# Transformer block and mixer block on one core: the grid pooling of the D rows moves from GpSimd to VectorE, and two small steps of the A rows move to ScalarE

## The chip, the cores and the metric

The kernel runs on one core of one Trainium2 chip. The metric is the device time of one execution in microseconds (us), here the median of three runs. Engines are named as the profile names them: PE is TensorE, DVE is VectorE, ACT is ScalarE, POOL is GpSimd, SP is the engine that issues the DMAs.

## What is computed

Two blocks in a row on one sequence of 1024 tokens, width 1024, all in float32. The first block is a feed-forward layer, an attention and state-space mixer, a second feed-forward layer and an embedding gate; the change does not touch it. The second block is the mixer that the change is about:

```
proj = h @ w_in                       # 11 slots of 512: va za bb bc bv zb ca cg zc dv zd
ya   = rglru(va)                      # A rows: two 4-tap convolutions, gates, two scans
yb   = bb * conv3(bc * bv)            # B rows
yc   = silu(ln(conv31(ca * sigmoid(cg)))) @ c_pw + c_pw_b    # C rows
p    = pool_grid(dv)                  # D rows: box mean over a 16 x 64 grid, minus the token
yd   = (p @ d_w + d_b) * d_scale      # per group of 128 channels
out  = concat(ya*silu(za), yb*silu(zb), yc*silu(zc), yd*silu(zd)) @ w_out

# pool_grid: channel group ct = 0..3 has a window w = 2, 4, 8, 16 in both directions
total = sum of g[r0:r1, c0:c1],  r0, r1 = clip(r - w/2), clip(r + w/2), same for columns
mean  = total / ((r1 - r0) * (c1 - c0));   result = mean - u

# rglru, per direction: r, ig = sigmoid(xc @ w + b); a = exp(-8 r softplus(-lam))
# b = sqrt(1 - a^2) * ig * xc;   h = a * h + b, forward and backward over the tokens
```

## The kernel before

Channels lie on the 128 partitions and tokens along the free axis, so a slot of 512 channels is four rows of 128 x 1024, and the function `mixer` of each engine loops over these with `ct` = 0 to 3. There is no scheduler: each engine's program is written out by hand, in the order in which its instructions run, and `Signal` objects (`mm` for PE, `ac` for ACT, `ve` for DVE, `po` for POOL) give the semaphore values to wait for. An engine that waits holds back everything that stands behind it in its program.

**PE.** A product of a float32 weight block with the activations is done as three products of split values (high and low part), 24 matmuls of 128x512 for each half (512 tokens) of a row. `plane` issues the two halves of one or more rows. For one ct the order is va, dv, cg (three rows, all first halves and then all second halves), ca, the gate products of direction 0 (`gates(0, ct)`, on XC0), bc, bv, the gate products of direction 1 (on XC1), bb, zb, za, the product `dw` of the pooled D rows (on DV), zd; then the next ct. For ct = 0 the first five rows come half by half (`first_planes`). After ct = 3 come four rows zc, and then the output products.

**PSUM banks.** The ring `banks` has eight banks, taken in PE's order, so a product waits for the reader of the product eight takes before it. What matters here: bb waits for the ACT copy of bc, zb for DVE's multiplication `pb` with bv, and the first half of zd waits for DVE's multiplication `bb` with the first half of bb.

**Weights.** Each weight unit (128 x 1024) is loaded to one of three RAW slots by SP, then ACT writes the high half and DVE the low half of one of five WS slots (`halves`, called by `release`). The low half of a unit is made at that place of DVE's program where the unit five before it is released; it waits for ACT's high half, and that for PE to be done with the unit five before. At the start of a ct from 1 on, DVE's program makes three of them in a row, for the units that follow va, dv and cg in their slots, and the last cannot be made before PE has ended the second half of cg. So DVE's work on a ct is held until then.

**DVE, one ct.** (1) The two 4-tap convolutions XC0 and XC1 of the A rows: a TENSOR_SCALAR for the first tap and three SCALAR_TENSOR_TENSOR. (2) UU, the product of ca and the gate of cg. (3) `convolve(n)`: the next n of the 31 taps of the C rows' convolution, each a SCALAR_TENSOR_TENSOR on CV (128x1024); the taps are filler, spread over the ct, and the rest follows at its end. (4) `gates(0, ct)`: GG, then a wait for ACT's exponential and tanh, RG = (x+1)*RG (`gv1`), x = 1-RG (`gv2`), RG = (RG-2)*RG (`gv3`), a wait for ACT's square root, GG = GG*RG; then the scan YY (`y1`). (5) five taps, weights, `pb`, weights, `gates(1, ct)`, five taps, the scan `y2`, YY + RG, the 3-tap convolution of the B rows, four taps, `bb`. (6) weights, the gate rows zb and za, eight taps, the bias and scale of `dw`, the gate rows zd, the rest of the taps.

**ACT, one ct.** Copies VA, DV and the bc row out of PSUM, sigmoids, in `gates` the exponential, the tanh and the square root, and the Silu of the z rows.

**POOL.** Its only work of note is the pooling of the D rows (function `gpsimd`, lines 2950 to 2991), once per ct, after ACT's copy of dv into DV. It zeroes the column borders of D0, copies DV between them, adds along columns by doubling (ct + 1 adds), then adds 2 * 2^ct shifted rows one after the other into a zeroed tile, multiplies by the two reciprocal counts and subtracts DV in place:

```
            for o in range(-hw_, hw_):
                lo_, hi_ = max(0, -o), min(16, 16 - o)
                e.wait_ge(po("col", ct, o - 1))
                if hi_ > lo_:
                    tt(dst[:, lo_:hi_, :], dst[:, lo_:hi_, :], src[:, lo_ + o:hi_ + o, :], ALU.add).then_inc(*po.inc("col", ct, o))
```

In the rows of the profile DVE's and ACT's instructions carry the lines of small helpers: L1826 is `tt` of DVE (TENSOR_TENSOR), L1830 and L1831 `ts` (TENSOR_SCALAR), L1834 `stt` (SCALAR_TENSOR_TENSOR), L1837 `scan`, L1048 `act`, L360 a matmul of PE, L2954 `tt` of POOL.

Of the kernel before, what the change touches and what calls it, by code (L numbers as in the profile page):

```python
# [142 lines left out]
def build(nc, t, plan):  # L143
# [900 lines left out]
    def scalar(e):  # L1044
# [593 lines left out]
        def mixer():  # L1638
            for ct in range(4):
                us = [w.take() for _ in range(3 if ct else 5)]  # L1640

# [20 lines left out]
                if ct:  # L1662
                    for h in range(2):
                        va_copy(h)
                        if h:
# [13 lines left out]
                else:  # L1679
# [141 lines left out]
    def vector(e):  # L1821
# [1594 lines left out]
```

## Time and profile before

| | before |
|---|---|
| median of three runs | 3488.39 us (3485.23 to 3490.15) |
| the profiled execution's own time | 3490.11 us |
| its span | 3487.2 us |
| TensorE clock granted, mean | 0.977 |
| PE busy | 3303.1 us, 95% |
| DVE busy | 1923.3 us, 55% |
| ACT busy | 1063.6 us, 30% |
| POOL busy | 146.8 us, 4% |

The page's shares are means over the whole program. The mixer is the stretch from about 2670 to 3250 us of the span, and there the engines stand otherwise, so it is read by its own timeline. In a timeline row the first number is the start in us from the span's start, the second the length, and xN says that N like instructions were merged; instructions of one engine overlap a little, so intervals between starts are used for sums. In square brackets stands the idle time of the engine ahead of the row and what ended it. The ct before which a time lies can be told from POOL's rows: its adds of ct = 1, 2 and 3 begin at 2816, 2947 and 3086 us.

### The profile page before, as it was taken

What the parts mean: (1) busy time and instruction counts of PE and PEld (TensorE: products, weight loads), DVE (VectorE), ACT (ScalarE), POOL (GpSimd) and SP (SyncE); (2) the same over time, 40 slices, a digit from 0 to 9 for tenths busy, and PEclk for the clock granted to TensorE, in tenths of its full rate; (3) what the DMA queues carried; (4) which work ended last, traced back from release to release, by engine and by line L of the source; (5) the groups of instructions that cost most, each with busy time, mean ns of one, the idle gap of its engine ahead of it and who ended that gap; (6) DMA issues with size and microseconds to landing.
All of it is one profiled execution on the core that took longest, in us unless ns stands there. A gap on an engine that the chain in (4) does not pass through costs nothing.

```text
span 3487.2 us, 37191 instructions
## 1 busy us (share of the span) xinstructions
PE 3303.1 (95%) x15338; PEld 2669.8 (77%) x15338; DVE 1923.3 (55%) x3176; ACT 1063.6 (30%) x1547; POOL 146.8 (4%) x72
## 2 busy tenths in 40 slices
PE   8999999999999999989999999999999899898897
PEld 7888888877987877777778888888676677676686
DVE  4323322266768678786542222222767777878535
ACT  3121121224232566563231111111444322322412
POOL 0000000000000000000000000000001031251000
PEclk9999999999999999999999999999999999998998
DMA  4211211212433430014111111111112111112141
GB/s 146 74 61 61 73 61 49 73 57 101 129 102 120 151 110 13 13 43 161 45 37 49 49 49 49 49 43 49 49 55 84 67 48 69 37 52 97 61 151 49
DMA packets 86872, 246.95 MB, mean 71 GB/s; under 512 B 8368, under 2 KB 22064, under 8 KB 85168
## 3 DMA queue, kind: packets, MB, share of 16 engines
q1 hardware_dynamic: 86704, 244.58, 20.2%
q8 instruction: 121, 1.98, 0.2%
q14 instruction: 47, 0.39, 0.0%
HBM read 200.51 MB, written 44.04 MB: 70 GB/s over the span
## 4 chain that ended last, share of the span: by engine, by line
PE 77%; DVE 16%; ACT 5%; issue 2%; DMA 1%; DVEq 0%; SPq 0%; ACTq 0%
PE PS L360 75%; DVE CV L1834 2%; PE PS L365 2%; DVE XC L1834 1%; DVE X L1834 1%; DVE WS L1826 1%; DVE HELD L1869 1%; ACT WS L1048 1%; DVE RG L1834 1%; DVE XS L1834 1%; DVE GG L1826 1%; ACT PT L1048 1%; DMA RAW<-in_W 1%; DVE TMP L1834 1%; ACT RG L1048 1%
## 5 line engine op out<-in xcount | busy, mean ns | idle before, releaser
L360 PE MATMUL PS<-XS,WS 128*128 128x512 f32 x8352 | 1963.6, 396 | 76.1 <-DVE TMP L1826 24.3
L360 PEld LDWEIGHTS PS<-XS,WS 128*128 128x128 f32 x8352 | 1587.3, 191 | 437.9 <-issue 87.3
L360 PE MATMUL PS<-HS,WS 128*128 128x512 f32 x2208 | 511.4, 392 | 8.7 <-DVE WS L1826 8.7
L360 PEld LDWEIGHTS PS<-HS,WS 128*128 128x128 f32 x2208 | 416.4, 189 | 98.6 <-issue 11.9
L1048 ACT ACTIVATE WS<-RAW 128x1024 fp32r<-128x1024 f32 x282 | 288.6, 1050 | 526.3 <-PE PS L360 439.1
L1826 DVE TENSOR_TENSOR WS<-RAW,WS 128x1024 fp32r<-128x1024 f32 x282 | 341.4, 1232 | 175.3 <-ACT WS L1048 175.1
L1826 DVE TENSOR_TENSOR TMP<-TMP,PS 128x512 f32<-128x512 f32 x112 | 76.5, 686 | 654.0 <-PE PS L360 645.7
L1048 ACT ACTIVATE TMP<-PS 128x512 f32<-128x512 f32 x184 | 108.8, 596 | 541.8 <-PE PS L360 478.6
L1834 DVE SCALAR_TENSOR_TENSOR X<-PS,X 128x512 f32<-128x512 f32 x160 | 110.0, 689 | 241.0 <-PE PS L360 240.5
L1048 ACT ACTIVATE HS<-TMP 128x512 fp32r<-128x512 f32 x88 | 55.6, 632 | 478.6 <-DVE TMP L1826 478.6
L1834 DVE SCALAR_TENSOR_TENSOR CV<-UU,COL,CV 128x1024 f32<-128x1024 f32 x120 | 163.6, 1363 | 3.6
L2961 POOL MEMSET D<- 128x16 f32 (+3 forms) x4 | 0.6, 154 | 2668.5 <-PE PS L360 2668.3
L360 PE MATMUL PS<-KH,QH 128*128 128x512 f32 x384 | 104.2, 407 | 0.3 <-DVE QH L1826 0.3
L1048 ACT ACT_TABLE_LOAD x58 | 74.4, 1283 | 96.6 <-DVE GG L1826 86.8
L1826 DVE TENSOR_TENSOR HS<-TMP,HS 128x512 fp32r<-128x512 f32 x88 | 60.9, 692 | 61.4 <-ACT HS L1048 61.4
L1826 DVE TENSOR_TENSOR PT<-PS,PT 128x512 fp32r<-128x512 f32 x128 | 82.1, 682 | 15.5 <-ACT PT L1048 15.2
L1048 ACT ACTIVATE PT<-PS 128x512 fp32r<-128x512 f32 x128 | 69.7, 595 | 56.0 <-PE PS L365 55.0
L360 PE MATMUL PS<-MH,WS 128*128 128x512 f32 x256 | 80.9, 394 | 0.0
L2500 DVE TENSOR_REDUCE COLB<-PS 128x1 f32<-128x1024 f32 x64 | 77.7, 1214 | 0.9 <-PE PS L360 0.5
L2954 POOL TENSOR_TENSOR D<-D,D 128x960 f32<-128x960 f32 (+8 forms) x30 | 78.0, 2599 | 2.4
L360 PEld LDWEIGHTS PS<-KH,QH 128*128 128x128 f32 x384 | 67.4, 189 | 11.6 <-ACT VH L1048 0.5
L360 PE MATMUL PS<-PT,VH 128*128 128x256 f32 (+1 forms) x512 | 69.8, 289 | 0.6 <-DVE PT L1826 0.6
(288 smaller groups left out, 2987.2 us busy)
## 6 DMA issues: line engine op xcount, KB each, us to landing
RAW<-in_W SPq DMA_DIRECT2D x286, 512.0 KB, 3.7
DC<-TMP SPq DMA_DIRECT2D x32, 256.0 KB, 4.2
X<-in_xT SPq DMA_DIRECT2D x8, 512.0 KB, 8.7
DX<-X SPq DMA_DIRECT2D x2, 2048.0 KB, 8.1
DCZ<-CA SPq DMA_DIRECT2D x8, 512.0 KB, 4.0
DGA<-TMP SPq DMA_DIRECT2D x16, 256.0 KB, 2.7
DGB<-TMP SPq DMA_DIRECT2D x16, 256.0 KB, 3.7
CZ<-DCZ SPq DMA_DIRECT2D x8, 512.0 KB, 6.2
```

Of the source, the lines that this page charges most:

```text
L360: done = d.matmul(out, l, r, start=first, stop=last)
L365: done = d.transpose(out, x, idn)
L1048: return d.activation(out, x, f, bias=bias, scale=scale)
L1826: return d.tensor_tensor(out, a, b, op)
L1834: return d.scalar_tensor_tensor(out=out, in0=a, scalar=s, in1=b, op0=op0, op1=op1)
L1869: d.reciprocal(out[:, 0:width], x).then_inc(*ve.inc("rs", name, h))
L2500: d.tensor_reduce(mx, PS[:, 2 * (n % 2):2 * (n % 2) + 2, :], AX.XY, ALU.max).then_inc(*ve.inc("mx", n))
L2954: return d.tensor_tensor(out, a, b, op)
L2961: d.memset(cur[:, :, 0:hw_], 0.0).then_inc(*po.inc("pad", ct, 0))
```

## The change

It has four parts.

- The pooling is DVE's, in new functions `pool_rows` and `pool_columns`, between the scan `y1` and the weights and `pb` of the ct. It doubles in both directions: ct + 1 adds over rows (with small copies for the rows at the edge) and ct + 1 over columns, then the same two multiplications and the subtraction. D0 and D1 become D[0] and D[1] of 1536 elements at slightly moved addresses. PE's `dw` and the next users wait for `ve("pl", ct)`.
- POOL only fills zeros into the rows outside the grid: 448 elements of D[0] for ct = 1, 2, 3, and 320 of D[1] for ct = 2, 3, when DVE has ended the pooling of the ct before.
- ACT computes the first taps of XC0 and XC1 (`first_taps`, a Copy with a scale), after its copy of the second half of VA.
- ACT computes `gv2` (an Identity with scale -1 and bias 1). DVE does one tap of the C rows meanwhile, in `gates`.

The taps of the C rows are dealt out anew: per ct 4, 1 (in gates 0), none beside the pooling, 1 (in gates 1), 6, 4, `bb`, 3, 6 after `dw`, and the last 6 after zd; before it was 4, 5, 5, 4, `bb`, 8, and the last 5.

```
@@ ScalarE
             act(RG[:], RG[:], ACT.Tanh, scale=GL[:, 8 + 4 * n + ct:8 + 4 * n + ct + 1]).then_inc(*ac.inc("gtanh", ct, n))
+            e.wait_ge(ve("gv1", ct, n))
+            act(XC[n][:], RG[:], ACT.Identity, bias=ones[:, 0:1], scale=-1.0).then_inc(*ac.inc("gv2", ct, n))
             e.wait_ge(ve("gv3", ct, n))
...
+                def first_taps():
+                    for n in range(2):
+                        e.wait_ge(ac("va", ct, 1), *([ve("y2", ct - 1)] if ct else spilled() + [ve("pad", "va")]))
+                        act(XC[n][:], VA[:, 3 * n:3 * n + 1024], ACT.Copy, scale=col("a_conv", 16 * n + ct)).then_inc(
+                            *ac.inc("xc0", n, ct))
@@ VectorE
-        def gates(n, ct):
+        def gates(n, ct, convolve):
...
-            ts(x, RG[:], -1.0, 1.0, ALU.mult, ALU.add).then_inc(*ve.inc("gv2", ct, n))
-            e.wait_ge(ve("gv2", ct, n))
+            convolve(1)
+            e.wait_ge(ve("gv1", ct, n), ac("gv2", ct, n))
             stt(RG[:], RG[:], 2.0, RG[:], ALU.subtract, ALU.mult).then_inc(*ve.inc("gv3", ct, n))
...
+        def pool_rows(ct):
...
+            for q in range(ct):
+                s, lo_ = 1 << q, 1 - (2 << q)
+                if q:
+                    e.wait_ge(ve("pr", ct, q - 1), *[po("pad", ct, j) for j in range(min(ct, 2))])
+                    tt(rows(q + 1, lo_, 16 - s), rows(q, lo_, 16 - s), rows(q, lo_ + s, 16), ALU.add).then_inc(*ve.inc("prm", ct, q))
+                    d.tensor_copy(rows(q + 1, 16 - s, 16), rows(q, 16 - s, 16)).then_inc(*ve.inc("pr", ct, q))
+                else:
+                    e.wait_ge(ac("dv", ct, 1), ve("pl", ct - 1))
+                    tt(rows(1, 0, 15), own[:, 0:15, :], own[:, 1:16, :], ALU.add).then_inc(*ve.inc("prm", ct, 0))
+                    d.tensor_copy(rows(1, -1, 0), own[:, 0:1, :]).then_inc(*ve.inc("pra", ct, 0))
+                    d.tensor_copy(rows(1, 15, 16), own[:, 15:16, :]).then_inc(*ve.inc("pr", ct, 0))
...
+            d.memset(cur[:, :, 0:hw_], 0.0).then_inc(*ve.inc("pc0", ct, 0))
+            d.memset(cur[:, :, hw_ + 64:cw], 0.0).then_inc(*ve.inc("pc0", ct, 1))
+            mid = cur[:, :, hw_:hw_ + 64]
+            if ct:
+                tt(mid, rows(ct, -hw_, 16 - hw_), rows(ct, 0, 16), ALU.add).then_inc(*ve.inc("pc", ct, -1))
...
+        def pool_columns(ct):
...
+            for q in range(ct + 1):
...
+                e.wait_ge(ve("pc", ct, q - 1))
+                tt(dst[:, :, 0:width], src[:, :, 0:width], src[:, :, 1 << q:(1 << q) + width], ALU.add).then_inc(
+                    *ve.inc("pc", ct, q))
+                me, other = other, me
...
+            tt(dst, dst, rc, ALU.mult).then_inc(*ve.inc("mean", ct, 0))
+            e.wait_ge(ve("mean", ct, 0))
+            tt(dst, dst, cc, ALU.mult).then_inc(*ve.inc("mean", ct, 1))
+            e.wait_ge(ve("mean", ct, 1))
+            tt(DV[:], me[:, 0:1024], DV[:], ALU.subtract).then_inc(*ve.inc("pl", ct))
@@ VectorE, mixer
                 convolve(4)
-                gates(0, ct)
+                gates(0, ct, convolve)
...
-                convolve(5)
+                pool_rows(ct)
+                pool_columns(ct)
                 release(w.take())
...
-                gates(1, ct)
-                convolve(5)
+                gates(1, ct, convolve)
+                convolve(6)
...
-                convolve(8)
+                convolve(3)
...
+                convolve(6)
                 gate_rows("zd", ct, lambda h: ve("dw", ct, h), lambda h: tmp("dh", ct, h))
@@ GpSimd
+        for ct in range(1, 4):
+            e.wait_ge(ve("pl", ct - 1))
+            d.memset(D[0][:, 0:448], 0.0).then_inc(*po.inc("pad", ct, 0))
+            if ct > 1:
+                d.memset(D[1][:, 0:320], 0.0).then_inc(*po.inc("pad", ct, 1))
```

How the instructions stand, first on DVE in ct = 1, from the first gate's `gv1` to `pb`. Names are those of the tiles (XC_143 is XC0, D_154 and D_155 the two pooling tiles), the numbers the shape. Before (helpers at L1826 to L1837):

```order
L1834 SCALAR_TENSOR_TENSOR RG<-XC_143,RG 128x1024 [waits activation_done]
L1831 TENSOR_SCALAR XC_143<-RG 128x1024 [waits vector_done]
L1834 SCALAR_TENSOR_TENSOR RG<-RG 128x1024 [waits vector_done]
L1826 TENSOR_TENSOR GG<-GG,RG 128x1024 [waits activation_done]
L1837 SCALAR_TENSOR_TENSOR YY<-XC_143,COLB,GG 128x1024 [waits vector_done]
L1834 SCALAR_TENSOR_TENSOR CV<-UU,COL,CV 128x1024
L1834 SCALAR_TENSOR_TENSOR CV<-UU,COL,CV 128x1024 [waits vector_done] x4
L1826 TENSOR_TENSOR WS<-RAW,WS 128x1024 [waits weight_hi_done]
```

And after the scan YY of ct = 1 in the changed program (helpers at L1834 to L1845):

```order
L1834 TENSOR_TENSOR D_154<-DV 128x960
L2722 COPY D_154<-DV 128x64
L2723 COPY D_154<-DV 128x64
L2726 MEMSET D_155 128x16x2 [waits pool_done,vector_done]
L2727 MEMSET D_155 128x16x2
L1834 TENSOR_TENSOR D_155<-D_154 128x16x64
L1834 TENSOR_TENSOR D_154<-D_155 128x16x67 [waits vector_done]
L1834 TENSOR_TENSOR D_155<-D_154 128x1024 [waits vector_done]
L1834 TENSOR_TENSOR D_155<-D_155,CNT 128x1024 [waits vector_done] x2
L1834 TENSOR_TENSOR DV<-D_155,DV 128x1024 [waits vector_done]
L1834 TENSOR_TENSOR WS<-RAW,WS 128x1024 [waits weight_hi_done]
```

The five taps that stood ahead of the weights have gone from this place, and the whole pooling stands there, seven adds and multiplications of about 1024 elements and four small instructions. On ACT, the gates of direction 0 of ct = 1 in the changed program:

```order
L1047 ACT_TABLE_LOAD [waits vector_done]
L1047 ACTIVATE XC_143<-RG,COLB 128x1024 [waits activation_done]
L1047 ACTIVATE RG<-RG,COLB 128x1024 [waits activation_done]
L1047 ACTIVATE XC_143<-RG,ones 128x1024 [waits vector_done]
L1047 ACT_TABLE_LOAD
L1047 ACTIVATE RG<-RG 128x1024 [waits vector_done]
```

The fourth row is new; the two table loads are those that stood there before, and no other was added.

## Rows read from the trace of the kernel before

**Rows 1.** The page, busy time of the engines over the whole span.
```profile
PE 3303.1 (95%) x15338; PEld 2669.8 (77%) x15338; DVE 1923.3 (55%) x3176; ACT 1063.6 (30%) x1547; POOL 146.8 (4%) x72
```

**Rows 2.** Timeline of PE: in each ct, the gates, `dw`, and zd's start.
```profile
2774.26 57.00 PE L360 MATMUL PS<-XS,WS 128*128 128x512 f32 x240 [5.25 <-DVE TMP L1826]
2835.53 6.22 PE L360 MATMUL PS<-XC,GW 128*128 128x512 f32 x8 [4.28 <-issue]
...
2899.47 1.88 PE L360 MATMUL PS<-DV,GW 128*128 128x512 f32 x4
2905.69 56.19 PE L360 MATMUL PS<-XS,WS 128*128 128x512 f32 x240 [4.34 <-DVE TMP L1826]
...
3043.44 57.24 PE L360 MATMUL PS<-XS,WS 128*128 128x512 f32 x240 [6.58 <-DVE TMP L1826]
...
3190.62 57.04 PE L360 MATMUL PS<-XS,WS 128*128 128x512 f32 x240 [8.12 <-DVE TMP L1826]
```

**Rows 3.** Timeline of ACT: cg's second half read, ct 1, 2, 3.
```profile
2820.41 0.60 ACT L1048 ACTIVATE TMP<-PS 128x512 f32<-128x512 f32 x1 [3.89 <-PE PS L360]
2831.35 1.06 ACT L1048 ACTIVATE WS<-RAW 128x1024 fp32r<-128x1024 f32 x1 [9.39 <-PE PS L360]
...
2951.03 0.60 ACT L1048 ACTIVATE TMP<-PS 128x512 f32<-128x512 f32 x1 [3.89 <-PE PS L360]
...
3089.84 0.60 ACT L1048 ACTIVATE TMP<-PS 128x512 f32<-128x512 f32 x1 [3.89 <-PE PS L360]
```

**Rows 4.** Timeline of POOL: column adds of ct 1, row adds, the last subtractions.
```profile
2816.76 4.85 POOL L2954 TENSOR_TENSOR D<-D 128x1072 f32<-128x1072 f32 x2
...
2840.03 3.25 POOL L2954 TENSOR_TENSOR DV<-D,DV 128x1024 f32<-128x1024 f32 x1
...
2955.59 23.43 POOL L2954 TENSOR_TENSOR D<-D,D 128x768 f32<-128x768 f32 x8
...
3145.01 3.25 POOL L2954 TENSOR_TENSOR DV<-D,DV 128x1024 f32<-128x1024 f32 x1
```

**Rows 5.** Timeline of DVE: ct 0 first, then ct 1, then one of ct 2.
```profile
2687.71 3.93 DVE L1834 SCALAR_TENSOR_TENSOR XC<-VA,COL,XC 128x1024 f32<-128x1024 f32 x3
...
2825.79 9.64 DVE L1834 SCALAR_TENSOR_TENSOR XC<-VA,COL,XC 128x1024 f32<-128x1024 f32 x3
...
2846.80 1.22 DVE L1826 TENSOR_TENSOR WS<-RAW,WS 128x1024 fp32r<-128x1024 f32 x1
...
2857.52 1.23 DVE L1834 SCALAR_TENSOR_TENSOR RG<-XC,RG 128x1024 f32<-128x1024 f32 x1 [3.74 <-ACT RG L1048]
2858.78 0.69 DVE L1831 TENSOR_SCALAR XC<-RG 128x1024 f32<-128x1024 f32 x1
2859.51 1.22 DVE L1834 SCALAR_TENSOR_TENSOR RG<-RG 128x1024 f32<-128x1024 f32 x1
...
2865.39 6.54 DVE L1834 SCALAR_TENSOR_TENSOR CV<-UU,COL,CV 128x1024 f32<-128x1024 f32 x5
...
2977.10 1.27 DVE L1826 TENSOR_TENSOR UU<-TMP,PS 128x512 f32<-128x512 f32 x2
```

**Rows 6.** Timeline of DVE: weights before `pb` of ct 0, first weights of ct 2.
```profile
2740.43 1.22 DVE L1826 TENSOR_TENSOR WS<-RAW,WS 128x1024 fp32r<-128x1024 f32 x1
...
2941.73 1.23 DVE L1826 TENSOR_TENSOR WS<-RAW,WS 128x1024 fp32r<-128x1024 f32 x1 [7.76 <-ACT WS L1048]
```

**Rows 7.** DVE's groups by shape, whole span: count, busy us, mean ns.
```profile
L1826 DVE TENSOR_TENSOR CA<-CIN,PW 128x576 f32<-128x576 f32 x16 | 12.1, 758 | 0.7 <-DVE TP L1826 0.2
L1826 DVE TENSOR_TENSOR YY<-YY,RG 128x1024 f32<-128x1024 f32 x4 | 4.9, 1224 | 0.1
L2253 DVE COPY BB<-TB 128x256 f32<-128x256 f32 x2 | 0.6, 294 | 0.1
```

**Rows 8.** Windows from zd's start of ct 2: busy times, then PEclk, the granted clock.
```profile
3043.00:3049.00 6.00, 5.56 (x13) 4.41 (x14) 6.00 (x9) 1.54 (x2) 0.00 (x0) 0.51 0.48 140
3056.00:3090.00 34.00, 34.00 (x152) 28.15 (x151) 17.89 (x18) 7.88 (x11) 4.78 (x3) 1.00 0.20 72
```

More of the change, by code:

```diff
@@ L233, in build @@
     SQ = [at(f"SQ{k}", 154 + 4 * k, [128, 512], F32) for k in range(8)]
-    GW = at("GW", 188, [128, 5, 128], F32)
+    GW = at("GW", 188.0625, [128, 5, 128], F32)
     HX = at("HX", 184, [128, 2, 512], F32)
@@ L244, in build @@
     PB = at("PB", 168, [128, 1026], F32)
-    DV = at("DV", 172.25, [128, 1024], F32)
-    D0 = at("D0", 176.25, [128, 1280], F32)
-    D1 = at("D1", 181.5, [128, 1280], F32)
+    DV = at("DV", 172.03125, [128, 1024], F32)
+    D = [at(f"D{j}", 176.03125 + 6 * j, [128, 1536], F32) for j in range(2)]
     CNT = at("CNT", 206, [128, 4, 80], F32)
@@ L941, in mixer @@
                     banks.take(use, (ve, *use))
-                    e.wait_ge(dma("gw")(ct), po("pl", ct), *banks.free(use))
+                    e.wait_ge(dma("gw")(ct), ve("pl", ct), *banks.free(use))
                     mms([(bank(*use), GW[:, 4, :], DV[:, half(h)], True, True)]).then_inc(*mm.inc(*use))
@@ L1666, in mixer @@
                             release(us[0])
+                            first_taps()
                         dv_copy(h)
@@ L1693, in mixer @@
                     va_copy(1)
+                    first_taps()
                     dv_copy(1)
@@ L2696, in gates, with rows @@
             tt(GG[:], GG[:], RG[:], ALU.mult).then_inc(*ve.inc("gb_", ct, n))
+        def pool_rows(ct):
+            own, hw_, cw = DV[:].rearrange("p (r c) -> p r c", c=64), 1 << ct, 64 + (2 << ct)
+            def rows(q, a, b):
+                return D[(q - 1) % 2][:].rearrange("p (r c) -> p r c", c=64)[:, 8 + a:8 + b, :]
+            for q in range(ct):
[9 more added lines that the diff above has]
+                    d.tensor_copy(rows(1, 15, 16), own[:, 15:16, :]).then_inc(*ve.inc("pr", ct, 0))
+            cur = D[ct % 2][:, 0:16 * cw].rearrange("p (r c) -> p r c", c=cw)
+            e.wait_ge(*([ve("pr", ct, ct - 1), po("pad", ct, 0)] if ct else [ac("dv", 0, 1)]))
+            d.memset(cur[:, :, 0:hw_], 0.0).then_inc(*ve.inc("pc0", ct, 0))
[3 more added lines that the diff above has]
+                tt(mid, rows(ct, -hw_, 16 - hw_), rows(ct, 0, 16), ALU.add).then_inc(*ve.inc("pc", ct, -1))
+            else:
+                d.tensor_copy(mid[:, 0:1, :], own[:, 0:1, :]).then_inc(*ve.inc("pc0", 0, 2))
+                tt(mid[:, 1:16, :], own[:, 0:15, :], own[:, 1:16, :], ALU.add).then_inc(*ve.inc("pc", 0, -1))
@@ new lines, in pool_columns @@
+        def pool_columns(ct):
+            me, other, cw = D[ct % 2], D[(ct + 1) % 2], 64 + (2 << ct)
+            width = cw
+            for q in range(ct + 1):
+                src = me[:, 0:16 * cw].rearrange("p (r c) -> p r c", c=cw)
+                if q < ct:
+                    width -= 1 << q
+                    dst = other[:, 0:16 * cw].rearrange("p (r c) -> p r c", c=cw)
+                else:
+                    width = 64
+                    dst = other[:, 0:1024].rearrange("p (r c) -> p r c", c=64)
+                e.wait_ge(ve("pc", ct, q - 1))
+                tt(dst[:, :, 0:width], src[:, :, 0:width], src[:, :, 1 << q:(1 << q) + width], ALU.add).then_inc(
+                    *ve.inc("pc", ct, q))
+                me, other = other, me
+            rc = CNT[:, ct, 0:16].unsqueeze(2).to_broadcast([128, 16, 64])
+            cc = CNT[:, ct, 16:80].unsqueeze(1).to_broadcast([128, 16, 64])
+            e.wait_ge(ve("pc", ct, ct), dma("cnt")("cnt"))
+            tt(dst, dst, rc, ALU.mult).then_inc(*ve.inc("mean", ct, 0))
[3 more added lines that the diff above has]
+            tt(DV[:], me[:, 0:1024], DV[:], ALU.subtract).then_inc(*ve.inc("pl", ct))
@@ L3180, in sync @@
             loads(242 + 10 * ct)
-        e.wait_ge(*[cat_in(row, h) for row in range(6) for h in range(2)], ve("bh", 3, 1), mm("dw", 3, 1), po("pl", 3))
+        e.wait_ge(*[cat_in(row, h) for row in range(6) for h in range(2)], ve("bh", 3, 1), mm("dw", 3, 1), ve("pl", 3))
         d.dma_start(RW[:], DC[0:6].rearrange("k p n -> p k n")).then_inc(*dma("rw").inc("rw"))
```

43 lines of the change are left out of this document (1 added, 42 removed).

## The prediction

> **What bounds the kernel now.** I read the page first: PE is busy 95% of the span, DVE 55%, POOL 4% [rows 1]. So most of the time is PE's, and only where PE stands still can a change on DVE or POOL be worth anything. PE's timeline through the mixer shows where that is [rows 2]: the start of zd waits for a DVE instruction on TMP (`bb`) in every ct, 5.25, 4.34, 6.58 and 8.12 us, and in ct 1 the gate products wait another 4.28 us. Each wait has a tail: behind the wait at 3043.44 the granted clock was 0.51 for 6 us, the lower level of 1.2 GHz, against 1.00 a little later [rows 8].
>
> Next, what makes DVE late. Call T the moment at which PE ends the second half of cg, seen as the ACT row that reads it: 2820.41, 2951.03 and 3089.84 for ct = 1, 2, 3 [rows 3]. DVE is held for that moment by the weights, so every ct starts from T. From T to zd's start it is 85.3 us in ct 1 (2905.69), 92.4 in ct 2 (3043.44) and 100.8 in ct 3 (3190.62) [rows 2, 3]. PE's work is the same in all three, and so is DVE's list of instructions. What grows is POOL's row: its pooling ends at 2843.3 in ct 1, and at 3148.3, 58 us after T, in ct 3 [rows 4]. The DVE rows beside it are slow: three taps of XC took 3.93 us in ct 0, ahead of POOL's pooling, and 9.64 us in ct 1 beside POOL's adds [rows 5], 3.2 us a tap instead of 1.3. Once POOL has ended, the weights take 1.22 us and five taps 6.54 again. The two UU products, one operand of which lies in PSUM, took 1.27 us together in ct 2 while POOL's row adds ran [rows 4, 5], no longer than 2 x 0.6. So it is a conflict over SBUF between the two engines, and PE's stalls are mostly its echo.
>
> Is that all of it? From T, a ct 1 with nothing slowed would run: T + 2.7 (weights done), two convolutions of 0.78 + 3.93 to T + 12.1, UU to T + 13.3; then, by the rows taken after POOL had ended, 10.72 from the weights (2846.80) to `gv1` (2857.52), 7.87 on to the scan's end (2865.39), 6.46 for five taps [rows 5], and 33.83 from the weights at 2740.43 to zd at 2774.26 [rows 2, 6]. That is T + 72.2. PE itself could be at zd at about T + 74: in ct 1 its `dw` ended at 2901.35, T + 80.9, less the 4.28 us stall and some 3 us of the lower clock behind it (6.22 us for the gates) [rows 2, 3]. The conflict thus holds zd back by 13.1, 20.2 and 28.6 us against DVE's own list, 61.9 together. The weights of ct 1 stand at T + 26.4 instead of T + 13.3, which is the same 13.1.
>
> **The change, part by part.**
>
> *POOL's adds go.* The 61.9 us of delay go with them. In ct 0 the conflict falls in a time in which DVE waits for PE anyway; nothing is booked there.
>
> *Pooling on DVE.* An add of 1024 elements takes 1.224 us and one of 576 0.758 [rows 7], so 1.04 ns per element and 0.16 fixed; with 0.04 between an instruction and one that waits for it (0.69 from 2858.78, next at 2859.51 [rows 5]) an add of n costs 1.04n ns + 0.20 us. ct 0 has 5 adds or multiplications with 5056 elements: 6.3 us. ct 1 has 7 with 7152: 8.8. ct 2 has 9 with 9408: 11.6. ct 3 has 11 with 12048: 14.7. Copies and fills number 3, 4, 5 and 6; a copy of 256 elements took 0.29 us [rows 7], these are mostly smaller, bounds 0.05 and 0.29, taken 0.15. P = 6.5, 9.4, 12.3 and 15.7 us, 43.9 in all, every one of them ahead of `bb`.
>
> The forms are rows of 64 at a pitch of up to 80, and the two multiplications repeat an operand. The row of CA, which has such repeated operands, pays the flat price, so I take that. The first column add of each ct reads one operand from an odd element on. The XC and CV taps do so too, at every other tap, and five of them still come to 1.31 each [rows 5]; I book nothing. The Trainium skill (Vector Engine (DVE) Microarchitecture Reference, the part on the SBUF access granule, adjacent pairs) says that a port keeps its full rate only with pairs that start on an 8-byte boundary, and gives 1.30 against 1.054 ns per column for odd starts on both sources; by it four adds of about 1070 elements would cost 1.1 us more in all, and the sum would be 3453.3 instead of 3452.2. The taps of this trace show no such thing for one source.
>
> *First taps on ACT.* DVE then needs 6 taps of 1.31 from T + 2.7, to T + 10.6, and UU to T + 11.8. But the next weights need ACT's high half of za, done at 2832.41 = T + 12.0 [rows 3]. So part A starts at T + 12.0; the two instructions saved are worth 1.3 us, not 1.6. On ACT the rows of a plane come some 5.4 us apart, and it idles 3.89 us ahead of the one for cg [rows 3], likewise ahead of the one for dv; two Copies of about 1.06 (the price of its weight row [rows 3]) fit, and that idle time is their cover.
>
> *`gv2` on ACT.* On DVE 0.73 us (2858.78 to 2859.51) are replaced by a tap of 1.31, so a gate's chain grows by 0.58, and a tap less remains for later. ACT's Identity takes 1.06 to 1.2 by its other rows and no table load was added, so it ends within the tap. If it did not, the gate would grow by the difference, 0.2 us at most, 1.6 for all eight.
>
> *Taps moved.* Between `y1` and `bb` stood 14 taps (5, 5, 4); now 1 and 6 and 4 beside `gates(1)`, 11. In the sum: five are replaced by P, and behind that one in the gate (counted) and one more in the six, +1.31. After `bb` there are 15 instead of 13, 2.6 us more. They lie ahead of the next weights, which had 7.76 us of idle time in front of them (2941.73 [rows 6]); that covers them. If it were used up, each us of overrun would delay the weights only; PE needs them much later.
>
> *POOL's fills* of zeros, 448 and 320 elements, come when DVE does weights and `pb`. Five short fills could slow a DVE row each; I bound it by 0 and 1 us and book none.
>
> **The sum.** From T to zd: 12.0 + 10.72 + 7.87 + 0.58 + P + 33.83 + 0.58 + 1.31 = 66.9 + P, so 76.3, 79.2 and 82.6 us. All are later than PE's T + 74, so DVE still sets zd. Gains: 85.3 - 76.3 = 9.0; 92.4 - 79.2 = 13.2; 100.8 - 82.6 = 18.2; together 40.4. In ct 0, where nothing was slowed on the path, P is worth the five taps it replaces (6.5 and 6.46), and 0.58 + 0.58 + 1.31 = 2.5 us are lost. Net 37.9. The clock's drop behind zd's wait stays as it is in all four. PE's other stalls, for XC0 at 2835.53 and for banks, lie inside T to zd and give nothing extra. The profiled execution of 3490.1 us becomes 3452.2. The median shown is 1.7 lower, so I say **3451 us**, 1.1% faster.
>
> **Rivals.**
>
> *No relief (slower).* If DVE's slow rows came from something other than POOL, say ACT's or the DMAs' traffic in the same stretch, the change would only lengthen DVE's list ahead of `bb`: 66.9 + P against 72.2, that is 4.1 + 7.0 + 10.4, and 2.5 in ct 0, +24.0 us: 3512. It decides when less than 24.0/61.9 = 39% of the relief comes. Against it: the rows turn fast within one instruction of POOL's end, in every ct. Chance 2%.
>
> *Dear adds (less gain, or slower).* If short rows at a pitch, or an odd start, cost a half more, P grows by 22 us: 3473. At 1.86 times the price, 2.3 us for 1024 elements, the gain would be gone. For it: no DVE row of before has just this form. Against it: the CA row, and the conflict is gone that made adds slow. Chance of over 3463: 9%, of reaching 3481: 2%.
>
> *More gain.* zd's wait in ct 1 would be 2.3 us by the sum, shorter than any wait behind which I read the drop. If the clock stays up there, and adds follow each other at 1.14 (the pitch of unlinked rows) instead of 1.24, it is 2.7 + 3 us less: 3445. Below T + 74 nothing is to be had, so the floor is 61.9 less 5.4 (3 x 1.8) less 2.5: 3434. Chance of under 3444: 9%.
>
> **How the numbers follow.** The forecast's own range: adds shorter by 3 us and the clock 3 us on one side; on the other 10% on P (4.4), small instructions at 0.29 (2.5), late `gv2` (1.6) and fills (1). That is 3445 to 3460; chance 78%, which with the rivals' leaves 2% for what I don't see. With part of both neighbours, 3443 to 3463 holds 8 in 10. A measurement of this kernel tells about 0.2%, 7 us, from no change. Slower by more than that takes the no-relief case or adds at over twice the price: 3%. Within it: 2%. Faster: 95%.
>
> **What would show it.** DVE's XC taps in ct 1 to 3 at 1.3 us each, in place of 3.2. From T to zd 76, 79 and 83 us. The pooling on DVE 9.4, 12.3 and 15.7 us. PE's waits ahead of the gate products gone, and of its waits in ct 3 only that at zd left, near 9 us (82.6 - 74), longer than before in spite of the gain. ct 0 2.5 us longer. The sum is wrong if T to zd shrinks by the same amount in all three, if DVE waits for ACT at `gv3` or for its first taps, or if DVE reaches the weights at the next T late.

## The result, and the profile after

The changed kernel takes 3446.74 us (median of 4 runs, 3445.02 to 3447.07), the kernel before in the same comparison 3488.77 (3485.23 to 3490.15): a ratio of 0.9879 [0.9867, 0.9891], 42.0 us less. The forecast was 3451 us, within 3443 to 3463. The profiled execution took 3445.02 us with a span of 3443.2 and a mean granted clock of 0.982.

The page after, busy time of the engines (for before: [rows 1]):

```profile
PE 3289.3 (96%) x15338; PEld 2662.5 (77%) x15338; DVE 1888.1 (55%) x3210; ACT 1081.2 (31%) x1563; POOL 2.2 (0%) x9
```

POOL's 146.8 us have shrunk to 2.2. DVE took over some 42 us of pooling, gave ACT steps that had kept it busy for 21.3 us before, and is 35.2 us less busy in all: 35.2 + 42 - 21.3, so of the busy time of the steps that it kept some 56 us had been lost to POOL. The two groups that show it, of the changed kernel by shape (count, busy us, mean ns):

```profile
L1842 DVE SCALAR_TENSOR_TENSOR CV<-UU,COL,CV 128x1024 f32<-128x1024 f32 x120 | 154.0, 1283 | 3.3
L1842 DVE SCALAR_TENSOR_TENSOR XC<-VA,COL,XC 128x1024 f32<-128x1024 f32 x24 | 30.5, 1283 | 3.8 <-ACT XC L1047 3.2
```

and the same two of the kernel before, where the XC taps took twice as long on the mean:

```profile
L1834 DVE SCALAR_TENSOR_TENSOR CV<-UU,COL,CV 128x1024 f32<-128x1024 f32 x120 | 163.6, 1363 | 3.6
L1834 DVE SCALAR_TENSOR_TENSOR XC<-VA,COL,XC 128x1024 f32<-128x1024 f32 x24 | 61.6, 2567 | 0.9
```

The timeline of ACT after, its reading of cg's second half, which is T for ct 1, 2 and 3 ([rows 3] for before):

```profile
2820.61 0.60 ACT L1047 ACTIVATE TMP<-PS 128x512 f32<-128x512 f32 x1 [3.89 <-PE PS L359]
...
2940.20 0.60 ACT L1047 ACTIVATE TMP<-PS 128x512 f32<-128x512 f32 x1 [3.89 <-PE PS L359]
...
3064.31 0.60 ACT L1047 ACTIVATE TMP<-PS 128x512 f32<-128x512 f32 x1 [3.89 <-PE PS L359]
```

and the timeline of PE after, zd's start in ct 0 to 3 and the gate products of ct 1 ([rows 2] for before):

```profile
2773.96 57.49 PE L359 MATMUL PS<-XS,WS 128*128 128x512 f32 x240 [7.33 <-DVE TMP L1834]
2831.29 3.59 PE L359 MATMUL PS<-XC,GW 128*128 128x512 f32 x8
...
2896.36 54.68 PE L359 MATMUL PS<-XS,WS 128*128 128x512 f32 x240 [1.85 <-DVE TMP L1834]
...
3018.86 56.29 PE L359 MATMUL PS<-XS,WS 128*128 128x512 f32 x240 [4.77 <-DVE TMP L1834]
...
3146.46 53.86 PE L359 MATMUL PS<-XS,WS 128*128 128x512 f32 x225 [8.26 <-DVE TMP L1834]
```

From T to zd it is now 75.75, 78.66 and 82.15 us in place of 85.3, 92.4 and 100.8. zd still waits for the same instruction, `bb` (TMP), in every ct. The gate products take 3.6 us with no wait ahead of them; before it was 6.22, 3.67 and 5.33 behind waits of 4.28, 3.20 and 2.89.

On DVE, the steps of ct 1 from the weights that follow `UU` to those that follow the pooling, and the pooling of ct 3 at the end (timeline, changed kernel):

```profile
2832.64 1.22 DVE L1834 TENSOR_TENSOR WS<-RAW,WS 128x1024 fp32r<-128x1024 f32 x1 [0.36 <-ACT WS L1047]
...
2843.36 1.23 DVE L1842 SCALAR_TENSOR_TENSOR RG<-XC,RG 128x1024 f32<-128x1024 f32 x1 [3.74 <-ACT RG L1047]
2844.51 1.27 DVE L1842 SCALAR_TENSOR_TENSOR CV<-UU,COL,CV 128x1024 f32<-128x1024 f32 x1
2845.89 1.22 DVE L1842 SCALAR_TENSOR_TENSOR RG<-RG 128x1024 f32<-128x1024 f32 x1
...
2851.76 1.13 DVE L1834 TENSOR_TENSOR D<-DV 128x960 f32<-128x960 f32 x1
...
2860.67 1.22 DVE L1834 TENSOR_TENSOR WS<-RAW,WS 128x1024 fp32r<-128x1024 f32 x1
...
3095.48 1.13 DVE L1834 TENSOR_TENSOR D<-DV 128x960 f32<-128x960 f32 x1
...
3110.77 1.22 DVE L1834 TENSOR_TENSOR WS<-RAW,WS 128x1024 fp32r<-128x1024 f32 x1
```

In starts: weights to `gv1` 10.72 us, `gv1` to the pooling 8.40, the pooling 8.91 in ct 1 and 15.29 in ct 3, and from 2860.67 to zd at 2896.36 it is 35.69.

The granted clock behind zd's wait, for 6 us of ct 1, 2 and 3 (windows; the numbers behind POOL's are the clock, the DMA share and GB/s):

```profile
2896.00:2902.00 6.00, 5.64 (x25) 4.70 (x26) 6.00 (x9) 1.55 (x2) 0.00 (x0) 1.00 0.43 146
3019.00:3025.00 6.00, 6.00 (x20) 4.78 (x21) 6.00 (x8) 1.54 (x2) 0.00 (x0) 0.73 0.58 183
3146.00:3152.00 6.00, 5.54 (x13) 4.41 (x14) 6.00 (x9) 1.54 (x2) 0.00 (x0) 0.50 0.46 141
```

In ct 3 the clock was at its lower level, 1.2 GHz, as in ct 2 of before [rows 8]. Behind the 1.85 us of ct 1 it stayed at the upper level, 2.4 GHz; before, behind 4.34 us, the same stretch read 0.72 (windows of the kernel before):

```profile
2905.00:2911.00 6.00, 5.31 (x17) 4.30 (x18) 6.00 (x9) 1.54 (x2) 0.00 (x0) 0.72 0.43 126
```

**Where the 44.0 us of span went.** Ahead of the mixer's ct 0 the profiled execution was 2.5 us earlier, which is not put down to the change: the profiled runs below, whose programs are the same up to there, differ by 5 us at that point. ct 0 from VA's second copy to zd is 2.2 us longer. T to zd is 9.5, 13.8 and 18.6 us shorter. From zd to the next T, with PE always busy, it is 46.65, 43.84 and 45.45 us in place of 46.16, 45.35 and 46.40, 2.0 us less in all. Behind zd of ct 3 it is the same within 0.2. With the signs: -2.5 + 2.2 - 41.9 - 2.0 + 0.2 = -44.0.

### The profile page after: what moved, and what is told of

The parts are those of the page before. It is cut to its first block, busy times and chain, and to the rows that moved or that the text cites. A ratio compares the mean times of both kernels' runs of the same rounds, so it can differ in the third digit from the quotient of the medians.

```text
span 3443.2 us, 37168 instructions
## 1 busy us (share of the span) xinstructions
PE 3289.3 (96%) x15338; PEld 2662.5 (77%) x15338; DVE 1888.1 (55%) x3210; ACT 1081.2 (31%) x1563; POOL 2.2 (0%) x9
## 4 chain that ended last, share of the span: by engine, by line
PE 79%; DVE 14%; ACT 5%; issue 1%; DMA 1%; DVEq 0%; SPq 0%; ACTq 0%
PE PS L359 77%; DVE CV L1842 2%; PE PS L364 2%; DVE X L1842 1%; DVE WS L1834 1%; DVE HELD L1877 1%; DVE D L1834 1%; ACT WS L1047 1%; DVE XS L1842 1%; DMA RAW<-in_W 1%; ACT PT L1047 1%; DVE TMP L1842 1%; DVE HELD L1834 1%; DVE RG L1842 1%; ACT TMP L1470 0%
## 5 line engine op out<-in xcount | busy, mean ns | idle before, releaser
L1834 DVE TENSOR_TENSOR TMP<-TMP,PS 128x512 f32<-128x512 f32 x112 | 76.5, 686 | 654.0 <-PE PS L359 645.7
L1834 DVE TENSOR_TENSOR WS<-RAW,WS 128x1024 fp32r<-128x1024 f32 x282 | 338.3, 1221 | 164.6 <-ACT WS L1047 164.4
L1842 DVE SCALAR_TENSOR_TENSOR CV<-UU,COL,CV 128x1024 f32<-128x1024 f32 x120 | 154.0, 1283 | 3.3
L1834 DVE TENSOR_TENSOR HS<-TMP,HS 128x512 fp32r<-128x512 f32 x88 | 60.9, 692 | 61.4 <-ACT HS L1047 61.4
L1834 DVE TENSOR_TENSOR PT<-PS,PT 128x512 fp32r<-128x512 f32 x128 | 82.1, 683 | 15.6 <-ACT PT L1047 15.2
L1842 DVE SCALAR_TENSOR_TENSOR X<-PS,MOD,X 128x512 f32<-128x512 f32 x48 | 35.6, 746 | 61.2 <-PE PS L359 56.2
L359 PEld LDWEIGHTS PS<-PT,VH 128*128 128x128 f32 (+1 forms) x512 | 62.0, 161 | 6.2 <-issue 5.1
```

The costliest lines, as they stand in the source:

```text
L359: done = d.matmul(out, l, r, start=first, stop=last)
L1842: return d.scalar_tensor_tensor(out=out, in0=a, scalar=s, in1=b, op0=op0, op1=op1)
```

## The experiments

All ratios are to the kernel before, run on the same chip beside it. "T to zd" is read in each trace as above.

**1. POOL does no pooling at all.** The kernel before, in which POOL's function is cut to one fill of eight elements per ct. The D rows are left unpooled, so that part of the computation is missing.

```
...
-            tt(DV[:], other[:, 0:1024], DV[:], ALU.subtract).then_inc(*po.inc("pl", ct))
+            d.memset(D0[:, 0:8], 0.0).then_inc(*po.inc("pl", ct))
```

> The kernel before, with the pooling left out altogether: POOL fills eight zeros per ct and the D rows go on unpooled; DVE's list is that of before. Conflict theory (POOL's adds slow DVE's rows): XC taps 1.3 us each in every ct, T to zd falls from 85.3, 92.4 and 100.8 us to PE's own 74 or so (DVE's own list is 72.2), zd's wait and the lower clock behind it vanish in ct 1 to 3: 3488.8 less 56 less up to 7, so 3425 to 3433 us. Rival (DVE's slow rows come from ACT's or the DMAs' traffic): taps stay at 3 us and the time at 3488.

3423.28 us, ratio 0.9811 [0.9796, 0.9825], 2 us under the range given. T to zd was 73.29 us in all three ct, and zd did not wait there (ct 1 and ct 3 shown):

```profile
2895.74 55.01 PE L360 MATMUL PS<-XS,WS 128*128 128x512 f32 x240
...
3130.66 55.01 PE L360 MATMUL PS<-XS,WS 128*128 128x512 f32 x240
```

So POOL's work was the only cause of the growth from ct to ct, and PE's own floor, the earliest start that PE's own work allows, is T + 73.3, where the prediction had T + 74.

**2. POOL kept busy beside the changed kernel.** POOL adds a scratch tile to itself for about as long as its pooling took.

```
+            e.wait_ge(ac("dv", ct, 1))
+            for k in range((6, 9, 14, 23)[ct]):
...
+                d.tensor_tensor(DUM[:], DUM[:], DUM[:], ALU.add).then_inc(*po.inc("du", ct, k))
```

> The changed kernel, and POOL besides adds a scratch tile of 880 elements to itself, 6, 9, 14 and 23 times in ct 0 to 3, each ct after ACT's copy of dv, about as long as its adds of before; nobody waits for it. Conflict theory: DVE's XC and CV rows beside it go back to about 3 us, T to zd from 76, 79 and 82 to about 90, 99 and 110, so 3446.7 plus 50 (40 to 62). Rival (other traffic, or the adds' own data path): unchanged, 3447.

3491.85 us, ratio 1.0007 [0.9997, 1.0016]: the whole gain is gone, with the programs of PE, ACT and DVE as in the changed kernel. The time is in the range given, but T to zd was 83.16, 91.54 and 103.02, shorter than the 90, 99 and 110 expected. The timelines of POOL and DVE in ct 3:

```profile
3087.06 54.73 POOL L3026 TENSOR_TENSOR DUM<-DUM 128x880 f32<-128x880 f32 x23 [75.88 <-ACT DV L1048]
```

```profile
3095.78 15.64 DVE L1843 SCALAR_TENSOR_TENSOR XC<-VA,COL,XC 128x1024 f32<-128x1024 f32 x6
3111.34 1.27 DVE L1835 TENSOR_TENSOR UU<-TMP,PS 128x512 f32<-128x512 f32 x2
...
3113.93 2.14 DVE L1839 TENSOR_SCALAR CV<-UU,COL 128x1024 f32<-128x1024 f32 x1
```

Six taps took 15.64 us in place of 7.76; the two UU products, with one operand in PSUM, took the 1.27 us that they always take. The scratch tile is touched by nobody else, so the data do not matter, only that both engines go to SBUF.

**3 and 4. The two small steps put back on DVE**, each alone, in the changed kernel: the first taps of XC, and `gv2` with its tap behind the gate.

```
-                    first_taps()
...
+                    ts(x, VA[:, o:o + 1024], col("a_conv", 16 * n + ct), None, ALU.mult).then_inc(*ve.inc("xc0", n, ct, 0))
```

```
-            convolve(1)
-            e.wait_ge(ve("gv1", ct, n), ac("gv2", ct, n))
+            e.wait_ge(ve("gv1", ct, n))
+            ts(x, RG[:], -1.0, 1.0, ALU.mult, ALU.add).then_inc(*ve.inc("gv2", ct, n))
+            e.wait_ge(ve("gv2", ct, n))
...
+            convolve(1)
```

> The changed kernel with the first taps of XC0 and XC1 back on DVE. By the sum: the weights of za start at T + 13.3 instead of T + 12.0, T to zd 1.3 us longer in ct 1, 2 and 3, nothing in ct 0: +3.9 us, 3450.6; if the longer wait at zd in ct 1 (1.85 to 3.1 us) brings the lower clock back there, 1.7 more, 3452.3. Rival (ACT's part is worth nothing, since DVE waits for ACT's high half of za anyway): 3446.7.

> The changed kernel with 1 - RG back on DVE (0.73 us) and the tap of each gate behind the gate instead of in it. By the sum each gate and tap together grow by 0.73 us, two per ct, all on the path to zd: +1.5 us in each ct, +5.8, so 3452.5; with the lower clock back in ct 1, 3454. Rival (ACT's round trip in the gate costs as much as it saves, the tap is not free): 3446 to 3448.

3451.00 us, ratio 0.9889 [0.9874, 0.9904], and 3453.59 us, ratio 0.9897 [0.9881, 0.9914], both near the forecasts and not at the rivals' 3447. In the traces T to zd grew by 1.14 us per ct with the first taps on DVE, and by 1.33 with `gv2` there. By the medians that is some 4 and 7 us, by the spans of the profiled executions, 3449.1 and 3449.5 beside 3443.2, some 6 each, of which 2.1 and 1.0 lie ahead of the mixer's ct 0. So these two parts are worth some 10 us of the 42; the rest is the pooling's. The lower clock came back in ct 1 in only one of them: behind a wait of 2.99 us at zd (first taps on DVE) the granted clock stayed at 1.00, behind one of 3.19 (`gv2` on DVE) it read 0.72 over 6 us, and from zd to the next T it was 43.81 and 45.42 us.

**5. Six taps fewer ahead of `bb`.** The changed kernel without the six taps behind the second gates; they fall to the end of the ct, 12 in a row there.

```
                 gates(1, ct, convolve)
-                convolve(6)
```

> The changed kernel, with the six taps of the C rows that stand behind the second gates taken out of the path to zd; they fall to the end of the ct (12 taps there in place of 6). My theory: zd is set by DVE's list, so each of the six taps (1.31 us, 7.9 together) counts until PE's own floor is met, T + 73.3 as in the run with an idle POOL. The lists of ct 1, 2, 3 (75.75, 78.66, 82.15) then give 73.3, 73.3 and 74.3, ct 0 about 7 us, and the lower clock behind zd's waits (2.5 to 3 us each) goes with the waits: about 3418 us, 3414 to 3424. Rival: the six taps are only moved, DVE now reaches the weights at the next T late (they had some 7.8 us of idle time ahead of them, less 2.6 already used), every ct starts later by 3 us or more, and the time is 3430 to 3442. If the clock drop is not tied to these waits, 3426.

3418.85 us, ratio 0.9801 [0.9786, 0.9816]. T to zd 73.33, 73.33 and 74.47. The granted clock behind zd of ct 2, 0.73 in the changed kernel and 0.51 before:

```profile
3003.00:3009.00 6.00, 6.00 (x25) 4.43 (x24) 5.96 (x8) 1.55 (x2) 0.00 (x0) 1.00 0.77 253
```

From zd to the next T it was 43.98, 44.16 and 44.16 us, so in ct 2 1.3 us came back with the clock, and in ct 0, whose wait had been 7.33 us, 2.7. T itself was not delayed: the second of the three first weights still waited, 1.58 us in ct 1, behind the twelve taps.

```profile
2790.48 15.81 DVE L1842 SCALAR_TENSOR_TENSOR CV<-UU,COL,CV 128x1024 f32<-128x1024 f32 x12
2806.21 1.22 DVE L1834 TENSOR_TENSOR WS<-RAW,WS 128x1024 fp32r<-128x1024 f32 x1
2809.01 1.23 DVE L1834 TENSOR_TENSOR WS<-RAW,WS 128x1024 fp32r<-128x1024 f32 x1 [1.58 <-ACT WS L1047]
```

**6. The pooling earlier as well**, in the kernel of experiment 5: in ct 0 behind `UU`, ahead of the weights, in ct 1 to 3 its row part between the second and third of the first weights.

```
-                    release(*us)
+                    release(*us[:2])
+                    pool_rows(ct)
+                    release(us[2])
...
+                if ct == 0:
+                    pool_rows(0)
+                    pool_columns(0)
                 release(*us, u)
```

> The kernel of e5_six_taps_last, with the pooling earlier too: in ct 0 all of it ahead of the weights in which DVE waits for PE, in ct 1 to 3 its row part between the second and the third weights of the start, where DVE waits for PE's cg. Theory: ct 0's wait ahead of zb (6.09 us, and some 2.7 of lower clock behind it) goes, ct 3 reaches the floor of T + 73.3: 7 to 9 us less than e5_six_taps_last, about 3410 (3406 to 3416). Rival: the pooling in ct 0 delays the start of XC1 or UU by its own 6.2 us because that idle time is not free, and nothing is gained beyond the 1 us of ct 3: the same as e5_six_taps_last within 2 us.

3411.26 us, ratio 0.9781 [0.9765, 0.9798]. PE's 6 us wait for PB in ct 0 is gone, zd waits only there (2.76 us), and ct 3 is at the floor, T + 73.33.

**7. The same doubling, done by POOL.** The changed kernel with `pool_rows` and `pool_columns` moved to POOL's program as they are, and DVE's five taps back at their place.

```
-                pool_rows(ct)
-                pool_columns(ct)
+                convolve(5)
...
-                convolve(6)
+                convolve(4)
@@ GpSimd
+        pool_rows(ct)
+        pool_columns(ct)
```

> The changed kernel with the same doubling pooling done by POOL, at the place where POOL did its pooling before; DVE has its five taps back in the pooling's place. It tells the number of adds from the engine that does them. Theory (each microsecond of POOL's adds costs DVE about half a microsecond of its two-operand work): POOL has 5, 7, 9 and 11 adds and multiplications of some 1000 elements at 2.4 to 3.3 us, so it is busy about 17, 23 and 28 us in ct 1 to 3 in place of 25, 37 and 61. T to zd is then some 79, 82 and 85 us, 3458 (3450 to 3468), between the kernels before and after. Rival 1, the number of adds was the whole matter: no slower than the changed kernel, 3447 or less. Rival 2, any pooling on POOL costs the same: 3480 or more.

3456.87 us, ratio 0.9909 [0.9894, 0.9924], in the range given. T to zd was 79.25, 81.96 and 87.21, so fewer adds, with the two steps on ACT, gave 32 of the 42 us, and taking the adds off POOL 10 more, after what they cost DVE. The rows in ct 3, POOL's five adds and DVE's six taps beside them:

```profile
3078.72 15.86 POOL L2960 TENSOR_TENSOR D<-D 128x1024 f32<-128x1024 f32 x5
```

```profile
3074.25 18.05 DVE L1842 SCALAR_TENSOR_TENSOR XC<-VA,COL,XC 128x1024 f32<-128x1024 f32 x6
```

3.2 us an add and 3.0 us a tap. In ct 0, where DVE was idle but for one UU product, two of POOL's multiplications took 4.38 us, 2.2 each.

**8. POOL fills in place of adding.** Experiment 2 with 18, 27, 42 and 69 fills.

```
-                d.tensor_tensor(DUM[:], DUM[:], DUM[:], ALU.add).then_inc(*po.inc("du", ct, k))
+                d.memset(DUM[:], 0.0).then_inc(*po.inc("du", ct, k))
```

> The kernel of e2_pool_busy, with POOL filling its scratch tile with zeros in place of adding it to itself: 18, 27, 42 and 69 fills of 880 elements (some 0.85 us each), for about as long as the adds took. The result is untouched. It tells whether the conflict comes from POOL's reads or from any use of SBUF by POOL. Theory A, the two engines share the way to SBUF whatever POOL does: about as slow as with the adds, 3480 to 3492. Theory B, DVE's instructions with two operands in SBUF are slowed only when POOL also reads: 3447, as the changed kernel. I hold A for somewhat likelier, 3:2, although the change's own five fills of 0.37 to 0.48 us slowed no DVE row beside them.

3451.93 us, ratio 0.9895 [0.9881, 0.9910]. The theory I had held likelier fell. In ct 3, with POOL writing for 62 us on end:

```profile
3066.11 62.00 POOL L3026 MEMSET DUM<- 128x880 f32 x69 [76.46 <-ACT DV L1048]
```

```profile
3073.62 7.76 DVE L1843 SCALAR_TENSOR_TENSOR XC<-VA,COL,XC 128x1024 f32<-128x1024 f32 x6
...
3084.07 1.27 DVE L1839 TENSOR_SCALAR CV<-UU,COL 128x1024 f32<-128x1024 f32 x1
```

The taps are untouched, 7.76 us for six, so theory B holds for them. What is slower is another kind: the TENSOR_SCALAR with one operand (1.27 us, 0.75 in the changed kernel) and the small copies of the pooling (0.33 to 0.54 in place of 0.19 to 0.28). T to zd grew by 0.6, 0.7 and 1.2 us.

**9. POOL copies in place of filling**: one read and one write.

```
-                d.memset(DUM[:], 0.0).then_inc(*po.inc("du", ct, k))
+                d.tensor_copy(DUM[:], DUM[:]).then_inc(*po.inc("du", ct, k))
```

> The kernel of e8_pool_fills with each fill replaced by a copy of the scratch tile onto itself: POOL now reads one tile and writes it, as often as it filled before (18, 27, 42, 69 times, some 0.9 us each alone). It tells whether it is POOL's reading that slows DVE's instructions with two operands in SBUF. Theory A (the two engines take turns, one whole instruction each, whenever POOL reads): every such DVE instruction beside a copy waits for about one copy, 0.9 us, so the taps take some 2.0 to 2.3 us in place of 1.28, and since POOL is held up in turn its copies last longer than alone; delays of about 15 to 45 us per ct, in all 3500 to 3550. Theory B (it takes POOL's two-operand adds): taps at 1.3, time 3452 as with the fills.

3506.98 us, ratio 1.0049 [1.0034, 1.0064], 55 us more than with as many fills; that is theory A, in its range, with taps a little shorter than its 2.0 to 2.3 us. T to zd 84.36, 96.03 and 112.40. DVE in ct 3:

```profile
3098.82 11.22 DVE L1843 SCALAR_TENSOR_TENSOR XC<-VA,COL,XC 128x1024 f32<-128x1024 f32 x6
3109.96 1.27 DVE L1835 TENSOR_TENSOR UU<-TMP,PS 128x512 f32<-128x512 f32 x2
...
3112.80 1.41 DVE L1839 TENSOR_SCALAR CV<-UU,COL 128x1024 f32<-128x1024 f32 x1
```

and POOL in ct 3, one copy beside a tap, and two while DVE waited for ACT:

```profile
3103.45 1.80 POOL L3026 COPY DUM<-DUM 128x880 f32<-128x880 f32 x1
...
3122.48 1.91 POOL L3026 COPY DUM<-DUM 128x880 f32<-128x880 f32 x2
```

A copy alone takes 0.93 us (two in 1.91, with 0.06 between them) and beside the taps 1.80; a tap alone 1.28, and beside the copies six took 11.22, 1.87 each. Both engines advance at one step of about 1.86 us, each slowed by the other: they take turns.

**10. Taps in the gates' waits.** DVE waits 3.74 us for ACT's tanh in each gate; two taps fit in. Experiment 10 puts them there in the kernel of experiment 6, and none ahead of `bb`; experiment 11 in the changed kernel, with two in place of six behind the second gates.

```
             tt(GG[:], GG[:], x, ALU.mult).then_inc(*ve.inc("g1", ct, n))
+            convolve(2)
             e.wait_ge(ac("gtanh", ct, n))
...
-                convolve(6)
+                convolve(2)
```

> The kernel of e6_pooling_earlier, with two taps in each of the two gates at the place where DVE waits 3.74 us for ACT's tanh, and none between the B rows' convolution and bb: T to bb is four taps (5.2 us) shorter in every ct. ct 1 to 3 are at PE's floor already; in ct 0 the last wait ahead of zd (2.76 us) goes. Theory: 3 us less than e6_pooling_earlier, 3408 (3406 to 3411); with nothing gained the wait has moved to bb's other inputs. Two taps take 2.6 us, so neither gate should end later.

> The changed kernel with one edit: of the six taps behind the second gates four stand in the gates instead, two in each wait of 3.7 us for ACT's tanh. The number of taps ahead of bb and behind it stays as it is, so this costs the later part nothing. DVE's list is 5.2 us shorter in every ct: T to zd 73.3, 73.5 and 77.0, ct 0 5.2 less (zd's wait there 2.1 in place of 7.3), and the lower clock behind the waits of ct 1 and 2 gone: 2.4 + 5.2 + 5.2 + 5.2 and some 3 to 5 of clock, about 3425 (3421 to 3431). If filling the wait delays gv1, that is if two taps and their start do not fit in 3.74 us, the gain is smaller by the overrun, eight times.

Experiment 11: 3425.59 us, ratio 0.9814 [0.9798, 0.9831]. T to zd 73.33, 73.40 and 76.87, and 5.4 us less in ct 0. `gv1` of ct 2 comes 4.96 us after GG, as in the changed kernel, with 1.23 us of the wait still left:

```profile
2953.10 1.22 DVE L1834 TENSOR_TENSOR GG<-GG,XC 128x1024 f32<-128x1024 f32 x1
2954.23 2.60 DVE L1842 SCALAR_TENSOR_TENSOR CV<-UU,COL,CV 128x1024 f32<-128x1024 f32 x2
2958.06 1.23 DVE L1842 SCALAR_TENSOR_TENSOR RG<-XC,RG 128x1024 f32<-128x1024 f32 x1 [1.23 <-ACT RG L1047]
```

Experiment 10: 3409.87 us (3405.12 to 3410.14), ratio 0.9768 [0.9753, 0.9782]. zd waits in no ct; in ct 0 it starts 73.3 us after VA's copy, in experiment 6 it was 76.7. That much is in the traces; by their ratios the two kernels cannot be told apart. Both beat the changed kernel, by some 36 us. From zb of ct 0 to zd of ct 3 PE's timeline has then no wait of 1 us or more.

## Why the prediction was right

**DVE's list sets zd, and POOL's adds stretched it.** Right, from both sides: without POOL's pooling the delay is gone (experiment 1), with other adds of about the same length it is back (experiment 2), and the rival of no relief is out. It had been put from rows that turned fast when POOL ended and from UU's unslowed rows.

**The sum, 66.9 + P.** Term by term in ct 1: to the weights 12.0, measured 12.03; to `gv1` 10.72, measured 10.72; the gate 7.87 + 0.58, measured 8.40; the rest 33.83 + 0.58 + 1.31 = 35.72, measured 35.69. P: 6.5, 9.4, 12.3 and 15.7 us forecast, 6.2, 8.9, 11.8 and 15.3 measured. (For ct 0 the prediction's own prices give 5.26 + 5 x 0.20 + 3 x 0.15 = 6.7, not 6.5.) An add that the next one waits for had been priced right: the pooling's groups by shape have 1024 elements at 1.20 to 1.23 us and 1264 at 1.48. What was too dear is the add whose next instruction does not wait for it. The rest of the pooling in ct 1, between the rows at 2851.76 and 2860.67 shown above:

```profile
2852.82 0.19 DVE L2722 COPY D<-DV 128x64 f32<-128x64 f32 x1
...
2853.22 3.76 DVE L1834 TENSOR_TENSOR D<-D 128x1024 f32<-128x1024 f32 x3
2857.01 2.49 DVE L1834 TENSOR_TENSOR D<-D,CNT 128x1024 f32<-128x1024 f32 x2
2859.53 1.23 DVE L1834 TENSOR_TENSOR DV<-D,DV 128x1024 f32<-128x1024 f32 x1
```

In starts, the first add took 1.06 us where 1.20 was booked, and the subtraction 1.14 where 1.26 was; the five between them took 6.31, booked at 6.38. The small instructions, booked at 0.15 each, were too dear in ct 1 (0.40 us for four) and too cheap in ct 3 (1.18 for six, where 0.90 was booked), so there the adds, 14.12 us for 14.73, gave all of it. Together that is the 0.5 us per ct by which T to zd came out shorter than 76.3, 79.2 and 82.6. The odd start of one operand cost nothing: the add of 1072 elements took 1.275 us, and 1.04 x 1072 + 160 ns is 1.27. By the granule rule of the Trainium skill (Vector Engine (DVE) Microarchitecture Reference, section Measured stream behaviour on trn2, the SBUF access granule), which gives its dearer rate for odd starts on both sources, these adds could have cost more; with one source odd, this trace does not show it.

**"The clock's drop behind zd's wait stays as it is in all four."** This step was wrong in two ct. In ct 1 the wait was 1.85 us and the clock stayed up, which is 1.5 us from zd to T; in ct 2 it was down for half as long, 0.95 us. The rival of more gain had named the first; its other half, adds at 1.14, came only for the few that nothing waits for. In experiments 5 and 10, where zd waits for 0.58 us at most, the clock behind it reads 1.00 in all four ct. The length of zd's wait does not settle it alone: in experiment 11 the clock fell behind 2.02 us in ct 0 (0.72 over 6 us), in a ct in which PE had waited 5.95 us earlier, and stayed up behind 2.98 us in ct 3. What decides in between stays open.

**ct 0** lost 2.2 us where 2.5 were booked (2.7 with P put right), and the tail of taps was hidden as said. PE's stalls ahead of the gate products went, and ct 3's wait at zd was 8.26 us, near the 9 forecast, longer than before.

**First taps and `gv2` on ACT.** 1.14 us per ct measured where the sum had 1.3. `gv2` ended together with DVE's tap, both at 3089.49 us in ct 3, and `gv1` to `gv3` is 2.53 us, where 1.99 + 0.58 made 2.57. The timeline of ACT in ct 3:

```profile
3088.33 1.16 ACT L1047 ACTIVATE XC<-RG,ones 128x1024 f32<-128x1024 f32 x1 [1.29 <-DVE RG L1842]
```

**The size.** The profiled span fell by 44.0 us where the sum had 37.9. Of the 6.1 between them, 1.5 are T to zd (41.9 where the sum had 40.4), 0.3 ct 0, 2.0 the clock, and 2.5 the time ahead of the mixer, which varies from run to run; 0.2 are lost behind the last zd. By the medians it is 42.0 us, where the forecast had 37 (3488.4 to 3451).

**What was not said.** The prediction took "a conflict over SBUF" as one thing. It has two conditions (experiments 2, 8 and 9), and I had the wrong guess at one of them. It did not matter for the sum, since the change took POOL's adds away altogether, but it would for a change that gives POOL other work.

## What to carry to other kernels

Read the same instruction beside an idle and beside a busy POOL: if a two-operand form doubles in time there, count part of POOL's busy time as taken from DVE's critical path (in the kernel before, zd was held 12.0, 19.1 and 27.5 us over its floor of 73.3 while POOL was busy 27.1, 41.0 and 61.3 us), and ask for less of it before asking where it runs (the doubling, left on POOL, with the two steps on ACT gave 32 of the 42 us here). Then look for idle time in the engine that sets the end, not only for less work: six taps moved out of the way, or four of them put into waits for ACT, gave another 21 to 28 us at no cost. A wait of the matmul engine costs more than its length when the clock falls behind it: the stretch from zd to the next T then took 1.2 to 2.7 us longer here than with no wait ahead of zd. Behind waits of 1.85 and 2.99 us in ct 1 it took no longer, so read the granted clock behind a wait before booking this.

## What the runs showed of the hardware

POOL and DVE take turns in SBUF, by kind of instruction. With POOL reading (a copy), a DVE tap with two operands in SBUF took 1.87 us in place of 1.28 and the copy 1.80 in place of 0.93; with POOL's two-operand adds of 880 elements a tap took 2.6 us, and of 1024 elements 3.0. With POOL only writing, the taps stayed at 1.29. DVE's instructions with one operand in SBUF and the other in PSUM were never slowed (UU 1.27 or 1.28 us for two in every row shown here). DVE's one-operand TENSOR_SCALAR on 1024 elements went from 0.75 to 1.27 us beside fills, to 1.41 beside copies and to 2.14 beside adds. The Trainium skill (SBUF — State Buffer, section Who interferes with whom) says just this: a DVE instruction with two SBUF inputs contends with a GpSimd instruction that reads SBUF and not with one that only writes, and a DVE instruction in one of the 2-port modes, which copy and tensor_scalar can enter, contends with GpSimd. The traces agree in all four cases; that the 0.75 us rows run in such a mode is taken from their pace and not shown. The Trainium skill says there too that the engine that issues second is blocked for the whole of the other's instruction; the common step of 1.86 us is a little less than the sum of the two alone, 1.28 + 0.93 = 2.21, so here the turns overlap by some 0.35 us.
